# Second block of a two-block transformer: gate tiles between the heads' steps, and another order of work at the output projection

## What is computed

```
for l in range(DEPTH):                       # 2 layers
    x = x + 0.5 * swiglu(rms_norm_2(x, ffn1_norm[l]), ...)        # width 2816
    h = rms_norm_2(x, mix_norm[l])
    z = h @ w_in[l]
    qa, ka, va, qs, ks_, vs, zg = jnp.split(z, splits, axis=-1)
    # qa, ka, qs, ks_ normalised per head of 64
    o_na = neighbourhood_attention(qa, ka, va, na_rpb[l])         # 8 heads
    o_sw = sliding_window_gqa(qs, ks_, vs, t5_bias, sw_sink[l])   # 8 heads, 2 kv heads
    g = jax.nn.sigmoid(zg + b_gate[l])       # two gates of width 1024
    merged = g[:, :, 0] * (o_na @ w_branch_na[l]) + g[:, :, 1] * (o_sw @ w_branch_sw[l])
    x = x + merged @ w_out[l]
    x = x + 0.5 * swiglu(rms_norm_2(x, ffn2_norm[l]), ...)
```

## Time and profile before

| | us |
|---|---|
| runs | 1824.42, 1832.38, 1837.05 (median 1832.38) |
| profiled execution, its time | 1833.09 |
| its span | 1831.3 |
| mean granted TensorE clock | 0.976 |
| busy: PE / PEld / DVE / ACT / POOL | 96% / 81% / 70% / 55% / 6% |

### The profile page before, as it was taken

How to read it: one execution, slowest core, us unless ns; L and a number is a source line. 1 busy time by engine, 2 the same in 40 slices (tenths; PEclk the granted TensorE clock), 3 DMA queues, 4 the chain that set the end, 5 groups by cost and what they waited for, 6 DMA issues and landing times.

```text
span 1831.3 us, 25437 instructions
## 1 busy us (share of the span) xinstructions
PE 1757.0 (96%) x9838; PEld 1491.8 (81%) x9838; DVE 1284.6 (70%) x2083; ACT 1002.4 (55%) x1672; POOL 113.4 (6%) x72
## 2 busy tenths in 40 slices
PE   7888999997999999999999989999999999989999
PEld 5758888885788888888786878888888787778888
DVE  5766775577477657876676778867886757677774
ACT  5564664457366445554457655545554456755552
POOL 0500000040000000000220000000000201000000
PEclk9989999997899999999999989999999999989999
DMA  7703555551265564555551345555555554145553
GB/s 271 219 1 138 192 200 184 196 195 47 84 220 197 194 209 181 193 188 208 226 183 48 117 160 184 188 207 200 188 184 207 210 184 158 47 145 179 192 197 139
DMA packets 62022, 313.97 MB, mean 171 GB/s; under 512 B 22685, under 2 KB 24353, under 8 KB 25294
## 3 DMA queue, kind: packets, MB, share of 16 engines
q1 hardware_dynamic: 60382, 303.93, 46.4%
q0 software_dynamic: 1232, 4.22, 0.8%
q10 hardware_dynamic: 288, 4.19, 0.6%
HBM read 311.25 MB, written 7.36 MB: 174 GB/s over the span
## 4 chain that ended last, share of the span: by engine, by line
PE 83%; DVE 8%; ACT 6%; issue 2%; SPq 1%; DMA 1%; DVEq 0%; ACTq 0%
PE acc L405 42%; PE acc L407 21%; DVE w_lo L380 4%; PE acc L394 3%; PE acc L396 3%; PE acc L395 3%; ACT w_hi L371 2%; PE tp L760 2%; PE acc L788 1%; PE acc L789 1%; PE sc L744 1%; PE acc L414 1%; PE acc L416 1%; PE acc L415 1%; PE sc L745 1%
## 5 line engine op out<-in xcount | busy, mean ns | idle before, releaser
L380 DVE TENSOR_TENSOR w_lo<-raw,w_hi 128x1024 fp32r<-128x1024 f32 (+1 forms) x564 | 692.4, 1235 | 321.5 <-ACT w_hi L371 319.5
L371 ACT ACTIVATE w_hi<-raw 128x1024 fp32r<-128x1024 f32 (+1 forms) x564 | 583.5, 1039 | 228.1 <-PE acc L407 121.6
L405 PE MATMUL acc<-act_a,w_hi 128*128 128x512 f32 x1552 | 547.3, 397 | 2.0 <-DVE w_lo L380 2.0
L407 PE MATMUL acc<-act_a,w_lo 128*128 128x256 f32 x1552 | 435.6, 281 | 0.0
L405 PE MATMUL acc<-hidden,w_hi 128*128 128x512 f32 x1216 | 423.5, 394 | 0.0
L405 PEld LDWEIGHTS acc<-act_a,w_hi 128*128 128x128 f32 x1552 | 292.6, 189 | 70.6 <-issue 2.2
L407 PE MATMUL acc<-hidden,w_lo 128*128 128x256 f32 x1216 | 339.1, 279 | 0.0
L407 PEld LDWEIGHTS acc<-act_a,w_lo 128*128 128x128 f32 x1552 | 294.3, 190 | 0.1
L405 PEld LDWEIGHTS acc<-hidden,w_hi 128*128 128x128 f32 x1216 | 227.9, 187 | 52.7
L562 ACT COPY part<-acc 128x256 f32<-128x256 f32 x272 | 101.1, 372 | 308.4 <-PE acc L407 307.4
L405 PE MATMUL acc<-act_b,w_hi 128*128 128x512 f32 x688 | 243.1, 399 | 0.0
(11 more groups left out here) (187 smaller groups left out, 2016.9 us busy)
## 6 DMA issues: line engine op xcount, KB each, us to landing
raw<-in_slabs SPq DMA_DIRECT2D x282, 1024.0 KB, 4.8
na_skew<-in_rpb SPq DMA_DIRECT2D x32, 128.0 KB
na_bias<-na_skew ACTq DMA_DIRECT2D x2, 2048.0 KB, 8.4
t_skew<-t_by_distance POOLq DMA_DIRECT2D x2, 1024.0 KB, 14.3
t_bias<-t_skew POOLq DMA_DIRECT2D x1, 2048.0 KB, 10.5
x_res<-in_x SPq DMA_DIRECT2D x1, 1024.0 KB, 5.1
out_x<-x_res SPq DMA_DIRECT2D x8, 128.0 KB, 4.9
prow<-in_prow SPq DMA_DIRECT2D x1, 518.0 KB
```

What stands on the lines that cost most here:

```text
L371: nc.scalar.activation(w_hi[u % RING][:, 0:n], raw[j % RAW][:, (u % 2) * HALF:(u % 2) * HALF + n], ACT.Copy).then_inc(s["unit_hi"], 1)
L380: nc.vector.tensor_tensor(w_lo[u % RING][:, 0:n], raw[j % RAW][:, (u % 2) * HALF:(u % 2) * HALF + n], w_hi[u % RING][:, 0:n].bitcast(F32), ...
L405: nc.tensor.matmul(bank[:, :], wh, src[:, c + i, :, :].rearrange("p i s -> p (i s)"), start=first and i == 0, stop=False, skip_group_check ...
L407: mm = nc.tensor.matmul(bank[:, S:2 * S], wl, src[:, c + i, 0, :], start=False, stop=last and i == n - 1, skip_group_check=True)
```

## The change

1. **Columns.** `w_in_2` is laid out as queries and keys of the neighbourhood heads, queries, keys and values of the window heads, and then the values of the neighbourhood heads. All that a norm needs lies in the first groups.
2. **Norms in two parts, inside the groups.** The neighbourhood part (2048 elements a row) is squared and reduced in group 2 and multiplied in group 3; the window part (1280) is squared and reduced in group 4 and multiplied beside head 1. GpSimd's power is taken twice, of 32 and of 20 columns.
3. **Transposes.** The seven fills go before group 4 (two), behind its first unit (two) and behind the first four scores (three); `scores` of the neighbourhood heads wait for four fills instead of seven.
4. **Gate tiles.** Not one stands ahead of the heads. Two stand behind the second and fourth `scores`, fourteen at the end of the steps in `GATE_STEPS` (all of 0 to 15 but 5 and 10), in banks 0 and 1. ScalarE splits and copies for them ahead of `exps(i)`, three steps later, and VectorE adds them behind `first(i)`.
5. **Output projection.** The tiles are made by `half_block`. VectorE adds one half bank in one instruction. ScalarE splits first and then does chunk and square of the tile before; VectorE adds x of the tile before, splits, and then does the square of tile n - 2 and the chunk of tile n - 1.
6. **Feed-forward's down projection**, wherever chunks follow: VectorE takes the square of the tile before ahead of the chunk, not its own square behind it.

```diff
-ZQA, ZKA, ZVA = 0, NAW, 2 * NAW
-ZQS = 3 * NAW
+ZQA, ZKA, ZQS = 0, NAW, 2 * NAW
 ZKS = ZQS + SWQW
 ZVS = ZKS + SWKVW
-ZG = ZVS + SWKVW
+ZVA = ZVS + SWKVW
+ZG = ZVA + NAW
...
+        def dve_next(dve, b, to, gain, n):
+            if n >= 1:
+                dve_square(dve, b, n - 1)
+            dve_chunk(dve, b, to, gain, n)
+            if n == DC - 1:
+                dve_square(dve, b, n)
...
+        def dve_x_half(dve, b, n, units):
+            bank = (b.mark("tile") - 1) % 4
+            dve.wait_ge(s["units_used"], units)
+            nc.vector.tensor_tensor(x[:, n, :], acc[bank][:, 0:S], x[:, n, :], ALU.add).then_inc(s["x_new"], 1)
+            b.mark("x_new")
+
+        def pe_tile_half(pe, b, src, released_by, need=None):
+            bank, before = tile_bank(b, released_by)
+            wait(pe, before)
+            u = pe_unit_in(pe, b)
+            for c in range(DC):
+                if need is not None:
+                    wait(pe, need(c))
+                mm = half_block(u, c, src, c, acc[bank][:, 0:S], c == 0, c == DC - 1)
+            mm.then_inc(s["units_used"], 1)
...
-                wait(pe, value(b, "heads_t", 7 if full else 2 if i < 4 else 4 if i < MOBA else 5))
+                wait(pe, value(b, "heads_t", (4 if i < NA else 7) if full else 2 if i < 4 else 4 if i < MOBA else 5))
...
+        FILLS2 = (0, 1, 4, 5, 2, 3, 6)
+        GATE_STEPS = (0, 1, 2, 3, 4, 6, 7, 8, 9, 11, 12, 13, 14, 15)
...
-            b.marks["tile"] = 2 + 4 * (b.at("tile") // 4 + 1)
-            for n in range(2 * DC):
-                pe_tile(pe, b, act_a, 1, (s["sum_ready"], b.mark("part")))
-                if n != HEADS_AFTER:
-                    continue
-                wait(pe, value(b, "normed", 1))
...
+                if g == len(G2) - 1:
+                    wait(pe, value(b, "normed", 1))
+                    fills.extend((f, heads_fill(b)) for f in FILLS2)
+                    turn_heads(fills[0:2])
...
+            def gate_tile():
+                k = b.mark("part")
+                pe_tile(pe, b, act_a, 1, (s["sum_ready"], k), None, k % 2)
+
+            def after_scores(i):
+                if i % 2:
+                    gate_tile()
+                if i == PROBS - 1:
+                    wait(pe, value(b, "normed", 2))
+                    turn_heads(fills[4:7])
+
+            pe_heads(pe, b, HEADS2, after_scores, lambda i: gate_tile() if i in GATE_STEPS else None)
...
-                pe_tile(pe, b, act_a, 1, (s["x_new"], b.mark("x_new")), merged if n == 0 else None)
+                pe_tile_half(pe, b, act_a, (s["x_new"], b.mark("x_new")), merged if n == 0 else None)
...
+                if g == 2:
+                    act_split(act, b, b.unit - n + RING)
+                    wait(act, value(b, "z_act", g))
+                    wait(act, value(b, "z_dve", g))
+                    nc.scalar.activation(sq_na[:, :, :], z2[:, :, 0:2 * NAW], ACT.Square).then_inc(s["qsq_ready"], 1)
...
+            def beside(i):
+                if i in (1, 2) or i - 3 in GATE_STEPS:
+                    b.unit += 1
+                    act_split(act, b, b.unit + RING - 1)
+                    act_part(act, b, (b.at("part") + 1) % 2)
+                if i == 2:
+                    copies(fills[4:7])
...
             for n in range(DC):
                 b.unit += 1
-                b.mark("x_new")
                 act_split(act, b, b.unit + RING - 1)
-                act_chunk(act, b, act_b, gain, n)
-                act_square(act, b, n)
+                if n >= 1:
+                    act_new(n - 1)
+            act_new(DC - 1)
...
             for n in range(DC):
                 b.unit += 1
+                if n >= 1:
+                    dve_x_half(dve, b, n - 1, b.unit - 1)
                 dve_split(dve, b, b.unit + RING - 1)
-                dve_x(dve, b, 1.0, n)
-                dve_chunk(dve, b, act_b, gain, n)
-                dve_square(dve, b, n)
+                if n >= 1:
+                    dve_next(dve, b, act_b, gain, n - 1)
+            dve_x_half(dve, b, DC - 1, b.unit)
+            dve_next(dve, b, act_b, gain, DC - 1)
...
+            for k, m0, m1 in ((1, 0, QKN), (2, QKN, QKN + QKS)):
+                wait(pool, value(b, "qms_ready", k))
+                nc.gpsimd.tensor_tensor(rstd_h[:, m0:m1], msq[:, m0:m1], half[:, m0:m1], ALU.pow)\
+                    .then_inc(s["qrs_ready"], 1)
```

More of the change, by code:

```diff
@@ L600, in dve_down @@
                 if to is not None:
[L601 to L602 removed]
+                    dve_next(dve, b, to, gain, n)
         X1, X2 = DC // 2 + DC, 3 * DC
@@ L718, in head_fills, with pe_heads @@
             return plan
-        def pe_heads(pe, b, heads, after_two=None, beside=None):
+        def pe_heads(pe, b, heads, after_scores=None, beside=None):
             fills = head_fills(b, heads)
@@ L770, in values @@
                     wait(pe, value(b, "z_act", 2 * len(G1)))
+                if i == 0 and full:
+                    wait(pe, value(b, "z_act", len(G2)))
+                    wait(pe, value(b, "z_dve", len(G2)))
                 v = [z[:, t, hd["v"]:hd["v"] + HD] for t in range(T)]
@@ L797, in pe_heads @@
                 scores(i)
-                if i == 1 and after_two is not None:
-                    after_two()
+                if after_scores is not None:
+                    after_scores(i)
             for i in range(n + 1):
@@ L927, in act_heads @@
                     copy(i - 3)
+                if full:
+                    beside(i)
                 if i < n:
                     exps(i)
-                if beside is not None:
+                if not full:
                     beside(i)
@@ L1531, in after, with turn_heads @@
                     pe_bcast(pe, b)
-            for g, (c0, w) in enumerate(G2):
-                pe_group(pe, b, w, len(wide_units("", c0, w)), group_banks(g),
-                         [value(b, "z_act", g + 1), value(b, "z_dve", g + 1)], need if g == 0 else None,
-                         after if g == 0 else None)
-            b.marks["tile"] = 2 + 4 * (b.at("tile") // 4 + 1)
-            for n in range(2 * DC):
-                pe_tile(pe, b, act_a, 1, (s["sum_ready"], b.mark("part")))
-                if n != HEADS_AFTER:
-                    continue
-                wait(pe, value(b, "normed", 1))
-                for f in range(7):
-                    bank, _, before = heads_fill(b)
+            def turn_heads(fills):
+                for f, (bank, _, before) in fills:
                     wait(pe, before)
@@ L1583, in act_layer2 @@
                     act.wait_ge(s["rstd_ready"], b.at("rsum"))
+                if g == len(G2) - 1:
+                    copies(fills[2:4])
                 act.wait_ge(s["units_used"], b.unit)
@@ L1655, in dve_layer2, with beside @@
                                         ALU.mult).then_inc(s["z_dve"], 1)
[L1656 to L1657 removed]
             part0 = b.at("part")
[L1659 removed]
+            def beside(i):
+                if i == 1:
+                    normalise(2, ZQS, QKN, QKN + QKS)
+                if i not in (1, 2) and i - 3 not in GATE_STEPS:
+                    return
+                n = b.at("part") - part0
                 b.unit += 1
                 dve_split(dve, b, b.unit + RING - 1)
[L1662 to L1675 removed]
+                dve_sum(dve, b, g2[:, n // 2, n % 2, :], (part0 + n + 1) % 2)
                 if n % 2:
@@ L1680, in dve_layer2 @@
                     nc.vector.tensor_tensor(gg, gg, r_of(2), ALU.mult).then_inc(s["zg_ready"], 1)
-            for f in range(7):
-                heads_fill(b)
             dve.wait_ge(s["t5_in"], 16)
             wait(dve, value(b, "bias_ready", 1))
-            dve_heads(dve, b, HEADS2)
+            dve_heads(dve, b, HEADS2, beside)
             dve_split(dve, b, b.unit + RING)
```

147 lines of the change are left out of this document (80 added, 67 removed).

## The result

The changed kernel took 1805.81 us (median of 4 runs, 1801.90 to 1808.14), the kernel before 1834.14 beside it (1824.42 to 1837.05): ratio 0.985, 95% interval 0.981 to 0.990. The forecast was 1804 in a range of 1794 to 1817. The profiled execution took 1808.14 us, 24.95 less than the one before.

A forecast was written before the change was run, and what follows sets the result against it. PE was taken as the only possible bound from gate tiles to branch, a ring off PE in the output projection. Output projection 15.8, clock 4.2 and heads 9 sum to 29.0; 1833.09 - 29.0 = 1804.1, predicted 1804 us, range 1794 to 1817.

The forecast's parts named there:

- Output projection: From branch end to end of the next tile: PE sets the pace, gain 7.9 us a layer, 15.8 in all.
- a ring: Output projection: split low part, x, chunk, square, split high part wait in a circle off PE, 3.85 us a tile.
- The form: Output projection tile as 24 matmuls of 256 columns: 2.88 us against 2.83, +0.05 a tile, 0.4 a layer.
- The half clock: Behind the output projection's next tile: PE no longer idles into half clock; at most 5.0 us, taken as 4.2.
- Gates and heads: First gate tile to first branch matmul: 8.4 us of slack a layer, 4.5 taken, 9 for two layers.
- the 4.9 to 5.2: Heads: length in us of a step with a gate tile that would show the prediction right.
- values 0.74 with nothing between: Heads: values need 0.74 us, not 1.01; perhaps 0.9 between other work, 2.5 a layer, half counted, 1.25.
- the entry into a gate tile: Heads: entering a gate tile from a small matmul costs about 0.08 us, 14 times, 1.1 a layer.
- the two steps without a gate tile: Heads, steps 5 and 10: `second` and `first` are waited for, 0.3 us each.
- only the output projection gains: Rival: gate tiles cost as much at their seams as they fill, taking the heads' 9 us; 1813 us, chance 0.10.
- The power holds VectorE: Rival: GpSimd's power delays group 2's second low split some 6 us, PE falls to half clock; 1813 us, chance 0.03.
- The scalar queue: Rival: a gate tile's end must precede the next head's exponentials, 2.4 us bare per gated step; 1871 us, chance 0.04.

The follow-up runs named there:

- the two halves of the part: Kernel before with only the new order of work at the output projection, 1805.91 us; with only its new form of tile (24 matmuls of 256 columns), 1825.47 us.

## Why the prediction was right, and where it wasn't

**Output projection: right in mechanism and in size.** 15.9 for 15.8. The argument that the order was a ring and that the new order has none is what the two halves of the part showed. The form was costed at +0.05 us a tile; it is 0.04 to 0.08. The half clock: 4.6 for 4.2, though the reason for taking less than 5.0, that the row sum's short matmuls don't scale, was wrong: they took 0.70 us at half clock (1073.41 to 1074.11) and 0.36 in the changed kernel (1064.52 to 1064.88).

**Gates and heads: right in sign, the term mis-sized.** The forecast had 4.5 us a layer; it is 1.1 where the clock fell as before, 1.7 without the projection groups. A step with scores and a gate tile took 5.34 us (947.87 to 953.21), beyond the 4.9 to 5.2 that were to be the sign of being right. The step that failed is "values 0.74 with nothing between", with half of the rest counted back. Values measured 1.01 in every step (1.08 in the last), 16.2 us where I had 13.1. The 0.74 of the earlier trace rows wasn't what values cost without a wait: it was the start of the next head's values inside the time of the last one's, seen where two heads stand one behind the other. The same trace has what let it start there, ScalarE's copy of the last head's probabilities:

```profile
1014.12 0.59 ACT L913 COPY prob_t<-tp 128x512 f32<-128x512 f32 x1 [0.20 <-PE tp L760]
```

It ends at 1014.71, and that head's values start at 1014.76. The change puts single heads between other work, where there is nothing to overlap with, and so these 3.1 us a layer were never to be had from it. The second error is the entry into a gate tile: 0.11 us on average for all sixteen (1.8 us), not 0.08 for fourteen (1.1); 0.7 us a layer. Against that transposes came 0.7 cheaper. Of the two steps without a gate tile, step 5 cost nothing and step 10 0.4 us (turn 0.83 instead of 0.49, scores 1.03 instead of 0.96), where 0.6 was counted.

**The total came out near in part by luck.** Profile against profile, the sum said 1804.1 and 1808.1 was measured: the heads' term fell 4.4 us short and the others came 0.5 over. Even this has 2.3 us from layer 1's wait and clock, which are no part of the change. The median, 1805.8, lies another 2.3 below the profiled execution. The rival "only the output projection gains", at 1813 and with a chance of 0.10, was about as near by the profile (4.9 off, the forecast 4.0). Its mechanism, seams that cost as much as they fill, is what the kernel with all tiles ahead showed.

**The power holds VectorE: no.** VectorE beside the power of 32 columns, which ran from 903.88 to 910.21:

```profile
903.71 2.41 DVE L381 TENSOR_TENSOR w_lo<-raw,w_hi 128x1024 fp32r<-128x1024 f32 x2
907.13 1.23 DVE L381 TENSOR_TENSOR w_lo<-raw,w_hi 128x1024 fp32r<-128x1024 f32 x1 [1.01 <-ACT w_hi L372]
```

Two splits in 2.41 us, one in 1.23: nothing held. The row decided rightly against the rule of the Trainium skill (GPSIMD Engine Reference, Specifications) for the power, while for the subtraction rule and rows agree.

**The scalar queue**: no wait in the changed kernel. That the distance of two gate tiles is the reason isn't shown: the kernel with pairs of tiles has a wait of 2.7 us, but on VectorE's queue, with the exponentials done 6 us earlier.

## What to carry to other kernels

When a chain of split, add, convert leaves the matrix engine waiting, write down which instruction of one tile waits for which of the same tile, on each in-order queue: moving work of tile n - 1 ahead of what tile n needs was worth 20 us here, and the form of the matmuls nothing on top of it. A duration that appears only where two like instructions meet is a sign of overlap, not of slack: try to make them meet everywhere (two heads of 64 columns side by side: 9 us a layer). And where VectorE is held beside a long GpSimd instruction, cut that into pieces, or move it, before looking for slack elsewhere.

## What was new of the hardware

- Two matmul groups of 64 weight columns, into output partitions 0 to 63 and 64 to 127 of one bank, took 1.02 us together and 1.01 each alone, if both heads' data were there.
- Beside GpSimd's subtraction even a VectorE instruction on 8 columns was held, so not only those with two large inputs; beside the power none was. Layer 1 of the changed kernel, timeline:

```profile
1439.91 1.23 DVE L381 TENSOR_TENSOR w_lo<-raw,w_hi 128x1024 fp32r<-128x1024 f32 x1 [1.67 <-ACT w_hi L372]
1441.05 9.02 DVE L1743 TENSOR_SCALAR neg_sink<-prow 128x8 f32<-128x8 f32 x1
...
1439.96 10.09 POOL L1815 TENSOR_TENSOR na_bias<-mask_n,na_bias 128x4096 f32<-128x4096 f32 x1 [3.15 <-DMA na_bias<-na_skew]
```

- Behind PE's waits of 1.68 to 2.06 us for that low part the granted clock stayed at 1.00 (2.4 GHz); behind those of 2.27 to 2.67 us it fell, and behind the longest, 2.68, it did not. So the same kernel can lose or keep some 1.6 us of clock in a layer, and with the wait's own length 2.3 us: 144.47 and 142.13 in the changed kernel, 142.13 and 144.30 in the one with the old output projection. What decides about the clock at the long waits stays open.
- The first part of the program, which the experiments on the second block leave as it is, ended between 860.9 and 875.4 us in these profiles. Differences of a few us must be read from stretches, not from times.
